# Moving the mLSTM branch's projection from Merge into the prelude of attention, with two of its splits on GpSimd

## The chip, the core and the metric

The kernel runs on one core of a Trainium2 chip. The metric is the device time of one launch in microseconds, as the median of several runs. The core has TensorE (matmuls; PE in the profile), VectorE (DVE), ScalarE (ACT), GpSimd (POOL) and SyncE (SP), which only issues transfers here. ScalarE and GpSimd issue transfers too, each into a queue of its own.

## The reference, cut to what matters

One layer of a hybrid backbone over T = 1152 tokens (128 context, 1024 latent), width D = 1024. Three branches (mLSTM, HGRN2, attention) each make an output of width 512 per token. Merge is then

```
proj_b  = einsum('blnw,nwd->blnd', branches, w_branch)   # n = 3 branches, w = 512, d = 1024
gates_b = sigmoid(bg)
merged  = sum_n(gates_b * proj_b)
x       = x + g1 * (merged @ w_out)
```

and an FFN follows. Everything is float32.

## The kernel before

The phases run one after the other, with a barrier of all engines between them: projection, mLSTM, HGRN2, attention (`attention`, L1452), Merge (`blend`, L1907), FFN (`ffn`, L2198). The two scans and attention write their outputs, features on the partitions, to `y_dram`, 4 x 128 rows for each branch.

**Three passes.** A float32 product is made of three matmuls on operands that are split in two: a high half, which is a copy rounded to TensorE's format (made by ScalarE), and a low half, the operand minus the high half (made by VectorE). `three_passes` (L52) issues high x high, high x low and low x high.

**Merge before.** `blend` multiplies the branches in three stages, n = 0, 1, 2, each of 8 tiles (t) of 128 output features. A tile is 3 column thirds (TH = 384 tokens) x 4 blocks of 128 inputs x 3 passes = 36 matmuls of 128x384, into three banks; two sets of banks alternate. TensorE may start tile m when VectorE has taken tile m-2 (`taken`). VectorE multiplies the banks by the tile's gate (L2088) and adds the product to `merged` (L2092, L2094). The gates are 24 transfers of 576 KB on GpSimd's queue (L1979) into a ring of four buffers, issued as buffers come free; ScalarE makes the sigmoid (L2011). Between tiles ScalarE and VectorE split the operands of the next stage (L1990, L1995, L2063, L2067), and in the last stage the output weights, in quarters (L2000, L2071). The loads come on SP's queue (L1950, L1954). The output projection and the residual follow.

**Stage 0's operands** are loaded in attention: SP issues four transfers of y (L1521) and two of weights (L1523) behind attention's own loads; ScalarE makes the six high halves first of all (L1707, L1710). VectorE makes the low halves in `ahead` (L1873, L1875), when the last query tile's second group begins, ahead of that group's normalisation.

**Attention before.** Its prelude is one chain. VectorE waits for four loads, squares and sums the keys (L1774 to L1778), GpSimd makes the power (L1542), VectorE scales the keys, turns them by the rotary table and splits them (L1785 to L1802). TensorE transposes them (L1588), and ScalarE evicts (L1715). Meanwhile VectorE norms the context's queries. These are transposed (L1568, L1573), then come the context's scores (L1602), their maxima on VectorE, exponentials on ScalarE (L1722), transposes of the probabilities (L1607), the eviction (L1725) and the context's outputs (L1613). Then four rounds: shift scores (L1626), each followed by a reduction on VectorE (L1858) that the next but one waits for at most. Then a loop over 8 query tiles of two groups of heads: nine key blocks each of scores (L1639, L1640), exponential (L1752) and values (L1649), with a normalisation (L1864, L1865) at the end. GpSimd makes the rotary products of the queries (L1556 to L1559) and the powers.

The engines' programs are written out by hand; semaphores carry the order.

Of the kernel before, what the change touches and what calls it, by code (L numbers as in the profile page):

```python
# [21 lines left out]
P = 128  # L22
# [1429 lines left out]
def attention(nc, g):  # L1452
# [14 lines left out]
    with Phase(nc, "att") as ph:  # L1467
# [27 lines left out]
        yt = ph.sb("yt", [P, 4, P])  # L1495
        names = ("load qload const knd kpow kout ktm kte qd qpow rope cpart qtm qte csmm cmx cex cptm cpte comm cdone "
                 "part s1 mx nm ptm pte s2 ex pv on yout kv dve mly mlw mlhi")
# [6 lines left out]
        use = lambda i, k: 2 + 5 * i + k  # L1504

        @block.sync
        def _(sp):
            tok = lambda c, w: g.tok_dram[:, c:c + w].rearrange("(t p) v -> p t v", p=P)
            with nc.allow_non_contiguous_dma(reason="rows of 64 values"):
# [12 lines left out]
            for b in range(2):  # L1522
                sp.dma_start(g.wraw[:, 2048 * b:2048 * b + 2048], io["w_branch"][b]).then_inc(sem["mlw"], 16)  # L1523
# [5 lines left out]
            with sp.Fori(0, 7) as i:  # L1529
                sp.wait_ge(sem["qd"], 4 * i + 8)  # L1530
                sp.dma_start(q[:].rearrange("p h d -> p (h d)"),
                             g.tok_dram[bass.ds(i * P + 2 * P, P), C_AQ:C_AQ + AH * HD]).then_inc(sem["qload"], 16)
            sp.wait_ge(sem["kout"], 32)

        @block.gpsimd
        def _(gp):
# [5 lines left out]
            gp.tensor_tensor(krs[:], kms[:], khalf[:], ALU.pow).then_inc(sem["kpow"], 1)  # L1542
            gp.wait_ge(sem["qd"], 3)
# [33 lines left out]
        def _(pe):  # L1577
            pe.wait_ge(sem["knd"], 6)

            n = 0  # L1580
            for part in range(2):
                rows = (P, H1)[part]
                for kv in range(KV):
                    for t0, nt in ((0, 4), (4, 4), (8, 2)):
# [6 lines left out]
                        n += 1  # L1591
            pe.wait_ge(sem["kte"], 12)
# [5 lines left out]
            mm.then_inc(sem["qtm"], 1)  # L1598
            pe.wait_ge(sem["qte"], 4)
# [4 lines left out]
            mm.then_inc(sem["csmm"], 1)  # L1604
            pe.wait_ge(sem["cex"], 8)
            for c in range(AH):
                mm = pe.transpose(ps[:, 6 + c // G, c % G * P:c % G * P + P], prc[:, c * P:c * P + P], g.ident[:])  # L1607
            mm.then_inc(sem["cptm"], 1)
            pe.wait_ge(sem["cpte"], 1)
# [5 lines left out]
            mm.then_inc(sem["comm"], 1)  # L1615

# [76 lines left out]
            for a in range(G):  # L1693
                shift_scores(0, 0, a)
            shifts(0, 0, 1)
            with pe.Fori(0, 7) as i:
# [7 lines left out]
        def _(act):  # L1704
            act.wait_ge(sem["mly"], 64)
            for k in range(4):
                act.activation(g.ys0[:, k, :], g.ys0[:, 4 + k, :].bitcast(F32), ACT.Copy).then_inc(sem["mlhi"], 1)  # L1707
            act.wait_ge(sem["mlw"], 32)
            for b in range(2):
                act.activation(g.wt[:, b, :], g.wraw[:, 2048 * b:2048 * b + 2048], ACT.Copy).then_inc(sem["mlhi"], 1)  # L1710
            for n in range(12):
# [3 lines left out]
                act.activation(kt[part][0:rows, kv, t0 * P:(t0 + nt) * P], ps[0:rows, n % 6, 0:nt * P], ACT.Copy).then_inc(sem["kte"], 1)  # L1715
            act.wait_ge(sem["qtm"], 1)
            for kv in range(KV):
                act.activation(qt[kv][:], ps[:, kv, :], ACT.Copy).then_inc(sem["qte"], 1)
                act.activation(qm[kv][0:H1, :], ps[0:H1, 2 + kv, :], ACT.Copy).then_inc(sem["qte"], 1)
            act.wait_ge(sem["cmx"], 1)  # L1720
            for c in range(AH):
                act.activation(prc[:, c * P:c * P + P], ps[:, 4 + c // G, c % G * P:c % G * P + P], ACT.Exp,  # L1722
                               bias=mxc[:, c:c + 1], scale=QS).then_inc(sem["cex"], 1)
            act.wait_ge(sem["cptm"], 1)
            act.activation(ptc[:].rearrange("p (a n) -> p a n", a=2), ps[:, 6:8, :], ACT.Copy).then_inc(sem["cpte"], 1)  # L1725
# [19 lines left out]
            def group(i, kv, more):  # L1745
# [3 lines left out]
                for j in range(NT):  # L1749
# [3 lines left out]
                    if j == 3 and kv == 0:  # L1753
                        output(use(i, 1), i)
                if more:
                    shifts(use(i, 2 if kv == 0 else 4), 1 - kv)

            queries(0, 0)
            shifts(1, 0)
            with act.Fori(0, 7) as i:  # L1760
# [5 lines left out]
            act.wait_ge(sem["yout"], 16 * 10)  # L1766

        @block.vector
        def _(v):
            link = Chain(v, sem["dve"])  # L1770
            wide = lambda x, n: x.unsqueeze(2).broadcast_to([P, n, HD])
            flat = lambda x: x.rearrange("p t h d -> p (t h) d")
            v.wait_ge(sem["load"], 64)
# [51 lines left out]

            norm_a(0)
# [80 lines left out]
def blend(nc, g):  # L1907
# [4 lines left out]
    with Phase(nc, "mrg") as ph:  # L1912
        ys = [g.ys0[:], g.zb[:, 0:8 * T].rearrange("p (k t) -> p k t", t=T)]
# [3 lines left out]
        wo = [[g.zb[:, 2 * D * k + D * n:2 * D * k + D * n + D] for n in range(2)] for k in range(4)]  # L1917
# [3 lines left out]
        g1 = g.zf[:, 8 * D:10 * D].rearrange("p (a n) -> p a n", a=2)  # L1921
        h = [g.ys0, g.xb]
# [7 lines left out]
        w_in = [ph.sem(f"w_in{i}") for i in range(2)]  # L1930
        bg_in = [ph.sem(f"bg_in{i}") for i in range(4)]
# [12 lines left out]
        def _(sp):  # L1944
            for n in (1, 2):
                if n == 2:
                    sp.wait_ge(mm_done, 8)
                for k in range(KB):
                    r = (KB * n + k) * P
                    sp.dma_start(ys[n % 2][:, KB + k, :].bitcast(F32), g.y_dram[r:r + P, :]).then_inc(y_in[k], 16)  # L1950
                for s in range(2):
                    if n == 2:
                        sp.wait_ge(w_lo, s + 1)
                    sp.dma_start(raw[s], io["w_branch"][2 * n + s]).then_inc(w_in[s], 16)  # L1954
            for k in range(KD):
                sp.wait_ge(w_lo if k < 4 else wo_lo, 3 + k // 2 if k < 4 else k - 3)
                sp.dma_start(quarter[k % 4], io["w_out"][k * P:k * P + P, :]).then_inc(wo_in[k % 4], 16)
            sp.wait_ge(mm_done, 16)
            for who in range(2):
                sp.dma_start(g1[:, who, :], g.gate_rows[who, 0:D].partition_broadcast(P)).then_inc(g_in, 16)  # L1960
            sp.wait_ge(m_lo, KD)
# [5 lines left out]
            sp.dma_start(g.zf[:, 5 * D + 5 * T:6 * D + 5 * T], io["w_ffn_out"][0:P, :]).then_inc(ahead, 16)  # L1967
# [3 lines left out]
            sp.wait_ge(ahead, 48)  # L1971

        @block.gpsimd
        def _(gp):
            gp.memset(half[:], -0.5).then_inc(pool, 1)
            for n in range(8 * NB):
                if n >= 4:
                    gp.wait_ge(taken, n - 3)
                gp.dma_start(bg[n % 4], g.bg_dram[n * P:n * P + P, :]).then_inc(bg_in[n % 4], 16)  # L1979
# [7 lines left out]
        def _(act):  # L1987
            def branch_hi(n, k):
                act.wait_ge(y_in[k], 16 * n)
                act.activation(ys[n % 2][:, k, :], ys[n % 2][:, KB + k, :].bitcast(F32), ACT.Copy).then_inc(y_hi, 1)  # L1990

            def weight_hi(n, s):
                act.wait_ge(w_in[s], 16 * n)
                act.wait_ge(mm_done, 8 * n + 4 * s - 4)
                act.activation(w[0][s], raw[s], ACT.Copy).then_inc(w_hi, 1)  # L1995

            def out_hi(k):
                act.wait_ge(wo_in[k % 4], 16 * (k // 4) + 16)
                act.wait_ge(mm_done, 16 if k < 4 else 20 if k < 6 else 24)
                act.activation(wo[k][0], quarter[k % 4], ACT.Copy).then_inc(wo_hi, 1)  # L2000

            def merged_hi(k):
                act.wait_ge(summed, k + 1)
                act.wait_ge(mm_done, 24)
                act.activation(h[0][:, k, :], g.merged[:, k, :], ACT.Copy).then_inc(m_hi, 1)

            for n in range(NB):
                for t in range(8):
                    m = 8 * n + t
                    act.wait_ge(bg_in[m % 4], 16 * (m // 4) + 16)  # L2010
                    act.activation(bg[m % 4], bg[m % 4], ACT.Sigmoid).then_inc(bg_sig, 1)  # L2011
# [37 lines left out]
            act.wait_ge(ahead, 48)  # L2049
# [7 lines left out]
        def _(v):  # L2057
            link = Chain(v, dve)

            def branch_lo(n, k):  # L2060
                x = ys[n % 2]
                v.wait_ge(y_hi, KB * (n - 1) + k + 1)
                v.tensor_tensor(x[:, KB + k, :], x[:, KB + k, :].bitcast(F32), x[:, k, :].bitcast(F32), ALU.subtract).then_inc(y_lo, 1)  # L2063

            def weight_lo(n, s):
                v.wait_ge(w_hi, 2 * (n - 1) + s + 1)
# [12 lines left out]
            for n in range(NB):  # L2079
                for t in range(8):  # L2080
                    m = 8 * n + t
                    if n and t == 0:
                        weight_lo(n, 1)
                    v.wait_ge(mm_done, m + 1)
                    v.wait_ge(bg_sig, m + 1)
                    into = g.merged[:, t, :]
                    dst = part[t % 2] if n else into
                    v.tensor_tensor(dst.rearrange("p (a n) -> p a n", a=3), ps[:, 3 * (t % 2):3 * (t % 2) + 3, 0:TH],  # L2088
# [67 lines left out]
        def _(pe):  # L2156
            for m in range(8 * NB):
                n, t, s = m // 8, m % 8, m % 8 // 4
                if n and t == 0:
                    pe.wait_ge(y_lo, KB * n)  # L2160
                if n and t % 4 == 0:
                    pe.wait_ge(w_lo, 2 * (n - 1) + s + 1)
                if m >= 2:
                    pe.wait_ge(taken, m - 1)
# [524 lines left out]
```

## Time and profile before

| | us |
|---|---|
| median of 3 runs | 2627.57 (2626.71 to 2628.74) |
| the profiled execution | 2627.34 |
| its span in the trace | 2625.4 |
| TensorE matmuls busy | 2452.9 (93%) |
| TensorE weight loads busy | 2263.3 (86%) |
| VectorE busy | 1180.9 (45%) |
| ScalarE busy | 680.8 (26%) |
| GpSimd busy | 140.3 (5%) |
| attention, first load to Merge's first matmul | 1176.4 to 1499.4 |

All times of rows are us from the span's start. Matmuls are pipelined, so a single one shows longer than the distance to the next. PEclk is TensorE's granted clock as a share of full speed.

### The profile page before, as it was taken

How to read it: one execution, taken by the hardware profiler on the slowest of the kernel's cores; microseconds unless marked ns; L12 is line 12 of the kernel's file. 1: busy time of each engine (PE TensorE's matmuls, PEld its weight loads, DVE VectorE, ACT ScalarE, POOL GpSimd, SP SyncE). 2: the span in 40 equal slices, each digit the busy share in tenths (PEclk: the TensorE clock that was granted, in tenths of full speed). 3: DMA queues.
4: the chain of work that ended last, by engine and by line, in shares of the span. 5: the costliest groups of instructions: out<-in, count | busy, mean ns of one | idle time of the engine just before them, and what ended most of it. 6: DMA issues, size and time to landing. Idle time of an engine off the chain costs nothing. (4 is left out here: it accounts for less than half of the span.)

```text
span 2625.4 us, 41733 instructions
## 1 busy us (share of the span) xinstructions
PE 2452.9 (93%) x17459; PEld 2263.3 (86%) x17459; DVE 1180.9 (45%) x1749; ACT 680.8 (26%) x1034; POOL 140.3 (5%) x179
## 2 busy tenths in 40 slices
PE   6999999997999789974999999988999999999998
PEld 4887689997999688973999899778999999999997
DVE  3331110102444555645555446554555555555555
ACT  3321111112233223323444333232211211111112
POOL 0000000001100000002111000010000000000000
PEclk8999999998999899995999999998999999999999
DMA  6225422215442532112000154223101110111012
GB/s 254 105 82 200 174 104 94 94 55 178 154 143 80 169 105 97 53 51 97 17 16 16 63 217 162 105 80 120 41 32 48 48 40 32 48 48 39 33 48 81
DMA packets 90780, 237.75 MB, mean 91 GB/s; under 512 B 11904, under 2 KB 49232, under 8 KB 80928
## 3 DMA queue, kind: packets, MB, share of 16 engines
q1 hardware_dynamic: 58464, 169.97, 18.6%
q10 hardware_dynamic: 28224, 50.74, 5.1%
q0 software_dynamic: 3968, 15.21, 1.7%
q8 instruction: 99, 1.62, 0.3%
q14 instruction: 25, 0.20, 0.0%
HBM read 179.13 MB, written 56.83 MB: 90 GB/s over the span
## 5 line engine op out<-in xcount | busy, mean ns | idle before, releaser
L55 PE MATMUL ps<-ys,wt 128*128 128x384 f32 x2688 | 703.3, 337 | 13.2 <-DVEq L2401 9.1
L55 PEld LDWEIGHTS ps<-ys,wt 128*128 128x128 f32 x2688 | 492.9, 189 | 31.0 <-DVEq L2401 9.5
L2354 DVE TENSOR_TENSOR merged<-merged,ps 128x512 f32<-128x512 f32 x378 | 259.5, 687 | 325.3 <-PE ps L55 322.1
L55 PE MATMUL ps<-xb,wt 128*128 128x384 f32 x1056 | 358.6, 340 | 0.0
L55 PE MATMUL ps<-zb 128*128 128x512 f32 x1056 | 298.2, 394 | 0.0
L55 PEld LDWEIGHTS ps<-xb,wt 128*128 128x128 f32 x1056 | 198.5, 188 | 17.2
L55 PEld LDWEIGHTS ps<-zb 128*128 128x128 f32 x1056 | 193.3, 188 | 16.6
L55 PE MATMUL ps<-prj_whi,h_hi 128*128 128x512 f32 (+1 forms) x432 | 165.0, 382 | 7.3 <-DVE h_lo L544 7.3
L55 PE MATMUL ps<-prj_wlo,h_hi 128*128 128x512 f32 (+1 forms) x432 | 162.7, 377 | 0.0
L55 PE MATMUL ps<-prj_whi,h_lo 128*128 128x512 f32 (+1 forms) x432 | 162.5, 376 | 0.0
L55 PE MATMUL ps<-h_hi,prj_whi 128*128 128x384 f32 x480 | 160.5, 334 | 0.8 <-ACT prj_tst L467 0.8
L55 PE MATMUL ps<-h_hi,prj_wlo 128*128 128x384 f32 x480 | 160.5, 334 | 0.0
L55 PE MATMUL ps<-h_lo,prj_whi 128*128 128x384 f32 x480 | 160.4, 334 | 0.0
L529 DVE TENSOR_TENSOR prj_wlo<-prj_raw,prj_whi 128x2048 fp32r<-128x2048 f32 (+1 forms) x22 | 48.1, 2199 | 240.3 <-ACT prj_whi L449 240.2
L1649 PEld LDWEIGHTS ps<-att_va,att_pt 128*128 128x128 f32 x1152 | 145.4, 192 | 6.3
L1649 PE MATMUL ps<-att_va,att_pt 128*128 128x65 f32 x1152 | 144.1, 270 | 0.0
L2286 ACT ACTIVATE zb<-zf 128x384 fp32r<-128x384 f32 x66 | 34.7, 526 | 395.9 <-DVE zf L2375 395.9
L1858 DVE TENSOR_REDUCE att_mx<-ps 128x1 f32<-128x1152 f32 x64 | 86.9, 1358 | 77.0 <-PE ps L1626 76.3
L55 PE MATMUL ps<-h_hi,hgr_gwhi 128*128 128x384 f32 x288 | 103.7, 360 | 12.7 <-DVE hgr_gwlo L687 12.4
L55 PEld LDWEIGHTS ps<-prj_whi,h_hi 128*128 128x128 f32 x432 | 82.6, 191 | 31.6 <-DVE h_lo L544 7.8
L1752 ACT ACTIVATE att_pt<-ps 128x512 f32<-128x512 f32 x144 | 83.5, 597 | 101.6 <-PE ps L1640 95.8
L55 PE MATMUL ps<-h_hi,mls_gwhi 128*128 128x384 f32 x288 | 101.2, 351 | 1.3 <-DVE mls_gwlo L687 1.3
(339 smaller groups left out, 3979.6 us busy)
## 6 DMA issues: line engine op xcount, KB each, us to landing
wraw<-in_w_ffn_in SPq DMA_DIRECT2D x22, 1024.0 KB, 4.8
prj_raw<-in_w_ada SPq DMA_DIRECT2D x16, 1024.0 KB, 6.0
xf<-bg_dram POOLq DMA_DIRECT2D x24, 576.0 KB, 4.1
tok_dram<-prj_tst ACTq DMA_DIRECT2D x45, 256.0 KB, 2.1
feat_dram<-prj_fst ACTq DMA_DIRECT2D x20, 576.0 KB, 2.8
zf<-in_w_ffn_out SPq DMA_DIRECT2D x22, 512.0 KB, 12.6
prj_raw<-in_w_tok SPq DMA_DIRECT2D x10, 1024.0 KB, 6.7
prj_raw<-in_w_feat SPq DMA_DIRECT2D x10, 1024.0 KB, 4.8
```

The costliest lines, as they stand in the source:

```text
L55: mm = pe.matmul(out, lhs[a], rhs[b], start=first and n == 0, stop=last and n == 2)
L529: v.tensor_tensor(w[1][b % 2][:, at], raw[u % NR][:, 0:width], w[0][b % 2][:, at].bitcast(F32), ALU.subtract).then_inc(lo_done, 1)
L1649: mm = pe.matmul(ps[:, OB, a * H1:a * H1 + H1], pt[j % 3][:, a * P:a * P + P], va[:, j, kv, :], start=False, stop=j == NT - 1 and a == G - 1)
L1752: act.activation(pt[j % 3][:], ps[:, ST + j % 3, :], ACT.Exp, scale=QS).then_inc(sem["ex"], 1)
L1858: v.tensor_reduce(mx[:, a % 2:a % 2 + 1], ps[:, 0:3, 0:TH], AX.XY, ALU.max).then_inc(sem["mx"], 1)
L2286: act.activation(a[0][s][:, t * TH:t * TH + TH], gate[:, t * TH:t * TH + TH], ACT.Copy).then_inc(a_hi, 1)
L2354: v.tensor_tensor(dst, dst, ps[:, bank, :], ALU.add).then_inc(added, 1)
```

## The change

Branch 0 (mLSTM) is multiplied in attention's prelude. The work is 24 blocks (`branch`), each one third of one tile: 12 matmuls into bank 6 or 7. Block u is tile 4*(u//12) + u%4, third u%12//4, so blocks 0 to 3 use third 0 of y and the first half of the weights, blocks 4 to 7 third 1, 8 to 11 third 2, and 12 to 23 the second half of the weights. ScalarE evicts each block (`store`) and issues its transfer to `b0_dram` (`put`). TensorE's blocks stand: 10 ahead of the key transposes, 2 behind them, 2 behind the query transposes, 3 behind the context's scores, 2 behind the probabilities' transposes, 1 behind the context's outputs and 4 between the rounds of shift scores. y's loads are by thirds; VectorE makes the low half of third 0 and of both halves of the weights, GpSimd those of thirds 1 and 2. The context's probabilities are transposed into banks 2 and 3 instead of 6 and 7.

Merge has 16 tiles instead of 24 (stages 1 and 2). In stage 1 VectorE first multiplies the stored product by its gate, then the banks by theirs, and adds. So GpSimd's queue brings two gates per tile there, and SP's a stored product. Branch 1's operands are loaded and split in attention: the loads behind the query loads, the high halves in the last query tile, the low halves in `ahead`, as before. The buffers of Merge and of FFN change places; FFN loads its first output weights itself, and multiplies by its gate row in two halves of 512.

```diff
 attention, sync:
+                branch_in(0)
+                branch_w(0)
                 sp.dma_start(kn[:]..., tok(C_AK, KV * HD)).then_inc(sem["load"], 16)
 ...
                 sp.dma_start(tab[:], io["rope"]).then_inc(sem["load"], 16)
+                branch_in(1)
+                branch_in(2)
+                branch_w(1)
 ...
-            for k in range(4):
-                sp.dma_start(g.ys0[:, 4 + k, :].bitcast(F32), g.y_dram[k * P:k * P + P, :]).then_inc(sem["mly"], 16)
-            for b in range(2):
-                sp.dma_start(g.wraw[:, 2048 * b:2048 * b + 2048], io["w_branch"][b]).then_inc(sem["mlw"], 16)
 ...
+            sp.wait_ge(sem["b0mm"], 24)
+            for k in range(4):
+                sp.dma_start(g.ys0[:, 4 + k, :].bitcast(F32), g.y_dram[(4 + k) * P:(5 + k) * P, :]).then_inc(sem["mly"], 16)
+            for b in range(2):
+                sp.dma_start(g.wraw[:, 2048 * b:2048 * b + 2048], io["w_branch"][2 + b]).then_inc(sem["mlw"], 16)
 attention, gpsimd, behind the keys' power:
+            for c in (1, 2):
+                gp.wait_ge(sem["b0yh"], c + 1)
+                at = slice(c * TH, c * TH + TH)
+                gp.tensor_tensor(g.ys0[:, 4:8, at], g.ys0[:, 4:8, at].bitcast(F32), g.ys0[:, 0:4, at].bitcast(F32),
+                                 ALU.subtract).then_inc(sem["b0yl"], 1)
 attention, tensor:
+            def branch(units):
+                for u in units:
+                    t, c = branch_unit(u)
+                    if u % 4 == 0 and u < 12:
+                        pe.wait_ge(sem["b0yl"], c + 1)
+                    if u % 12 == 0:
+                        pe.wait_ge(sem["b0wl"], u // 12 + 1)
+                    if u >= 2:
+                        pe.wait_ge(sem["b0ev"], u - 1)
 ...
+            branch(range(0, 10))
             pe.wait_ge(sem["knd"], 6)
 attention, scalar:
+            def store(units):
+                for u in units:
+                    act.wait_ge(sem["b0mm"], u + 1)
+                    if u >= 3:
+                        act.wait_ge(sem[f"b0out{u % 3}"], 16 * (u // 3))
+                    act.activation(b0st[u % 3][:], ps[:, 6 + u % 2, 0:TH], ACT.Copy).then_inc(sem["b0ev"], 1)
+                    if u:
+                        put(u - 1)
+            branch_hi(0)
+            weight_hi(0)
+            branch_hi(1)
+            branch_hi(2)
+            weight_hi(1)
+            store(range(0, 10))
 ... in group, behind exponential j:
+                    if isinstance(i, int) and kv == 0 and j in (1, 4, 6, 7):
+                        ahead((1, 4, 6, 7).index(j))
+                    if isinstance(i, int) and kv == 1 and j in (1, 4):
+                        ahead(4 + j // 4)
 attention, vector:
+            branch_lo(0)
+            weight_lo(0)
             v.wait_ge(sem["load"], 64)
 ...
+            weight_lo(1)
             norm_a(0)
 blend, sync:
+            for i in range(2):
+                sp.dma_start(done[i], g.b0_dram[i * P:i * P + P, :]).then_inc(done_in[i], 16)
+            ... y and weights of branch 2, the two gate rows g1
+            for i in range(2, 8):
+                sp.wait_ge(taken, 2 * i - 3)
+                sp.dma_start(done[i % 2], g.b0_dram[i * P:i * P + P, :]).then_inc(done_in[i % 2], 16)
 blend, vector:
+            for n in (1, 2):
                 for t in range(8):
+                    if n == 1:
+                        v.wait_ge(done_in[t % 2], 16 * (t // 2) + 16)
+                        v.wait_ge(bg_sig, m)
+                        v.tensor_tensor(into, done[t % 2], bg[(m - 1) % 4], ALU.mult).then_inc(taken, 1)
+                    v.wait_ge(mm_done, 8 * (n - 1) + t + 1)
 blend, tensor:
+            for m in range(16):
 ...
                 if m >= 2:
-                    pe.wait_ge(taken, m - 1)
+                    pe.wait_ge(taken, 2 * m - 2 if m < 10 else m + 7)
```

## Rows read from the trace of the kernel before

**Rows 1.** The page: span, engines' busy time and TensorE's line in 40 slices.

```profile
span 2625.4 us, 41733 instructions
PE 2452.9 (93%) x17459; PEld 2263.3 (86%) x17459; DVE 1180.9 (45%) x1749; ACT 680.8 (26%) x1034; POOL 140.3 (5%) x179
PE   6999999997999789974999999988999999999998
```

**Rows 2.** Windows: length, busy us of PE, PEld, DVE, ACT, POOL, granted clock, DMA share, GB/s.

```profile
1176.40:1200.70 24.30, 0.01 (x1) 0.01 (x1) 15.08 (x24) 7.36 (x6) 3.62 (x4) 0.50 0.79 262
1200.70:1242.50 41.80, 24.68 (x120) 20.68 (x121) 20.10 (x41) 13.92 (x29) 13.54 (x15) 0.62 0.09 22
1200.00:1210.00 10.00, 8.37 (x54) 8.13 (x55) 6.73 (x15) 6.90 (x13) 2.53 (x2) 0.73 0.16 41
1220.00:1230.00 10.00, 6.62 (x26) 5.12 (x24) 2.17 (x7) 1.62 (x2) 5.25 (x7) 0.50 0.10 26
1240.00:1250.00 10.00, 9.12 (x44) 7.51 (x44) 3.48 (x5) 3.58 (x6) 0.00 (x0) 0.69 0.01 2
```

**Rows 3.** Timeline of Merge: start, us, engine, line, operation; VectorE's products and TensorE's first stage.

```profile
1513.47 1.36 DVE L2088 TENSOR_TENSOR merged<-ps,xf 128x1152 f32<-128x1152 f32 x1 [1.89 <-PE ps L55]
...
1557.15 1.36 DVE L2088 TENSOR_TENSOR xf<-ps,xf 128x1152 f32<-128x1152 f32 x1 [1.86 <-PE ps L55]
...
1607.07 1.36 DVE L2088 TENSOR_TENSOR xf<-ps,xf 128x1152 f32<-128x1152 f32 x1 [1.10 <-PE ps L55]
...
1499.38 51.50 PE L55 MATMUL ps<-ys,wt 128*128 128x384 f32 x288 [4.09 <-PEq L75]
```

**Rows 4.** Timeline of attention's prelude: the keys' chain and the first group.

```profile
1183.02 1.36 DVE L1774 TENSOR_TENSOR att_k<-att_kn 128x1152 f32<-128x1152 f32 x1 [13.98 <-DMA att_tab<-in_rope]
...
1186.12 3.25 POOL L1542 TENSOR_TENSOR att_krs<-att_kms,att_khalf 128x18 f32<-128x18 f32 x1 [9.35 <-DVE att_kms L1778]
...
1189.48 1.36 DVE L1785 TENSOR_TENSOR att_kn<-att_kn,att_krs 128x1152 f32<-128x1152 f32 x1 [1.80 <-POOL att_krs L1542]
...
1200.69 4.53 PE L1588 MATMUL ps<-ident,att_kparthi 128*128 128x128 f32 x20 [30.40 <-DVE att_kpartlo L1802]
...
1241.80 1.09 PE L1568 MATMUL ps<-ident,att_qpart 128*128 128x128 f32 x4 [0.88 <-DVE att_qpart L1824]
```

**Rows 5.** Durations by line, ns min/median/max: the splits, GpSimd's multiplies, VectorE's beside the power.

```profile
L1707 ACT ACTIVATE ys<-ys x4: 1147/1147/1164, 1192.7 to 1195.9; 128x1152 fp32r<-128x1152 f32 x4
L1556 POOL TENSOR_TENSOR att_u<-att_qn,att_qtb x16: 735/740/745, 1211.7 to 1431.1; 128x256 f32<-128x256 f32 x16
L1782 DVE TENSOR_TENSOR att_qtab<-att_tab,att_grow x4: 418/425/426, 1185.9 to 1187.3; 128x256 f32<-128x256 f32 x4
```

**Rows 6.** Timeline in mLSTM: GpSimd's two selects and VectorE beside them; that operation's durations.

```profile
648.36 1.21 POOL L823 TENSOR_SCALAR_AFFINE_SELECT mls_ub<-mls_ub 128x1152 f32<-128x1152 f32 x1 [15.26 <-DMA mls_gn<-in_ml_g]
...
649.52 3.52 POOL L823 TENSOR_SCALAR_AFFINE_SELECT mls_ub<-mls_ub 128x1152 f32<-128x1152 f32 x1
...
648.53 3.45 DVE L1006 SCALAR_TENSOR_TENSOR mls_wsb<-mls_q,mls_wsb 128x2304 f32<-128x2304 f32 x1
651.90 1.22 DVE L1019 COPY mls_st<-mls_s 128x129 f32<-128x129 f32 x1
...
L1006 DVE SCALAR_TENSOR_TENSOR mls_wsb<-mls_q,mls_wsb x4: 2557/2558/3448, 648.5 to 811.6; 128x2304 f32<-128x2304 f32 x4
```

**Rows 7.** Merge's start: the sigmoids of gates 0 and 3, and a window of full queues.

```profile
1507.55 1.17 ACT L2011 ACTIVATE xf<-xf 128x1152 f32<-128x1152 f32 x1 [6.93 <-DMA xf<-bg_dram]
...
1519.59 1.17 ACT L2011 ACTIVATE xf<-xf 128x1152 f32<-128x1152 f32 x1 [1.55 <-DMA xf<-bg_dram]
...
1505.00:1510.00 5.00, 5.00 (x31) 5.00 (x30) 1.17 (x1) 2.23 (x2) 0.00 (x0) 1.00 1.04 426
```

**Rows 8.** Attention's tail: the fifth exponential, the weights' low halves, the last normalisation.

```profile
1485.86 0.60 ACT L1752 ACTIVATE att_pt<-ps 128x512 f32<-128x512 f32 x1 [0.76 <-PE ps L1640]
...
1481.84 5.16 DVE L1873 TENSOR_TENSOR ys<-ys 128x1152 fp32r<-128x1152 f32 x4
...
1486.91 4.49 DVE L1875 TENSOR_TENSOR wt<-wraw,wt 128x2048 fp32r<-128x2048 f32 x2
...
1493.93 0.18 DVE L1864 RECIPROCAL att_rs<-ps 128x4 f32<-128x4 f32 x1 [2.54 <-PE ps L1649]
```

More of the change, by code:

```diff
@@ L1495, in attention @@
         yt = ph.sb("yt", [P, 4, P])
+        b0st = [ph.sb(f"b0st{i}", [P, TH]) for i in range(3)]
         names = ("load qload const knd kpow kout ktm kte qd qpow rope cpart qtm qte csmm cmx cex cptm cpte comm cdone "
-                 "part s1 mx nm ptm pte s2 ex pv on yout kv dve mly mlw mlhi")
+                 "part s1 mx nm ptm pte s2 ex pv on yout kv dve mly mlw mlhi b0y0 b0y1 b0y2 b0w0 b0w1 b0yh b0wh b0yl b0wl b0mm b0ev b0out0 b0out1 b0out2")
         sem = {n: ph.sem(n) for n in names.split()}
@@ L1591, in _ @@
                         n += 1
+            branch(range(10, 12))
             pe.wait_ge(sem["kte"], 12)
@@ L1598, in _ @@
             mm.then_inc(sem["qtm"], 1)
+            branch(range(12, 14))
             pe.wait_ge(sem["qte"], 4)
@@ L1615, in _ @@
             mm.then_inc(sem["comm"], 1)
+            branch(range(19, 20))
             def queries(u, kv):
@@ L1694, in _ @@
                 shift_scores(0, 0, a)
+                branch(range(20 + a, 21 + a))
             shifts(0, 0, 1)
+            pe.wait_ge(sem["b0ev"], 24)
             with pe.Fori(0, 7) as i:
@@ L1715, in _ @@
                 act.activation(kt[part][0:rows, kv, t0 * P:(t0 + nt) * P], ps[0:rows, n % 6, 0:nt * P], ACT.Copy).then_inc(sem["kte"], 1)
+            store(range(10, 12))
             act.wait_ge(sem["qtm"], 1)
@@ L1719, in _ @@
                 act.activation(qm[kv][0:H1, :], ps[0:H1, 2 + kv, :], ACT.Copy).then_inc(sem["qte"], 1)
+            store(range(12, 14))
             act.wait_ge(sem["cmx"], 1)
@@ L1754, in group, with ahead @@
                         output(use(i, 1), i)
+                    if isinstance(i, int) and kv == 0 and j in (1, 4, 6, 7):
+                        ahead((1, 4, 6, 7).index(j))
+                    if isinstance(i, int) and kv == 1 and j in (1, 4):
+                        ahead(4 + j // 4)
                 if more:
                     shifts(use(i, 2 if kv == 0 else 4), 1 - kv)
+            def ahead(n):
+                if n == 0:
+                    act.wait_ge(sem["mly"], 64)
+                if n == 4:
+                    act.wait_ge(sem["mlw"], 32)
+                if n < 4:
+                    act.activation(g.ys0[:, n, :], g.ys0[:, 4 + n, :].bitcast(F32), ACT.Copy).then_inc(sem["mlhi"], 1)
+                else:
+                    b = n - 4
+                    act.activation(g.wt[:, b, :], g.wraw[:, 2048 * b:2048 * b + 2048], ACT.Copy).then_inc(sem["mlhi"], 1)
             queries(0, 0)
+            store(range(20, 24))
             shifts(1, 0)
+            put(23)
             with act.Fori(0, 7) as i:
@@ L1766, in _ @@
             act.wait_ge(sem["yout"], 16 * 10)
+            for i in range(3):
+                act.wait_ge(sem[f"b0out{i}"], 16 * 8)
         @block.vector
@@ L1920, in blend @@
         part = [g.xf[:, 4 + i, :] for i in range(2)]
-        g1 = g.zf[:, 8 * D:10 * D].rearrange("p (a n) -> p a n", a=2)
-        h = [g.ys0, g.xb]
+        done = [g.xf[:, 6 + i, :] for i in range(2)]
+        g1 = g.zf[:, 8 * T:8 * T + 2 * D].rearrange("p (a n) -> p a n", a=2)
+        h = [wide, g.xb]
+        g.h = h
         free = g.merged[:].rearrange("p k t -> p (k t)")
@@ L1930, in blend @@
         w_in = [ph.sem(f"w_in{i}") for i in range(2)]
+        done_in = [ph.sem(f"done_in{i}") for i in range(2)]
         bg_in = [ph.sem(f"bg_in{i}") for i in range(4)]
@@ L2003, in merged_hi, with gate @@
                 act.wait_ge(summed, k + 1)
-                act.wait_ge(mm_done, 24)
+                act.wait_ge(mm_done, 16)
                 act.activation(h[0][:, k, :], g.merged[:, k, :], ACT.Copy).then_inc(m_hi, 1)
-            for n in range(NB):
+            def gate(m):
+                act.wait_ge(bg_in[m % 4], 16 * (m // 4) + 16)
+                act.activation(bg[m % 4], bg[m % 4], ACT.Sigmoid).then_inc(bg_sig, 1)
+            for n in (1, 2):
                 for t in range(8):
-                    m = 8 * n + t
-                    act.wait_ge(bg_in[m % 4], 16 * (m // 4) + 16)
-                    act.activation(bg[m % 4], bg[m % 4], ACT.Sigmoid).then_inc(bg_sig, 1)
+                    if n == 1:
+                        gate(2 * t)
+                        gate(2 * t + 1)
+                    else:
+                        gate(16 + t)
                     if n < 2:
@@ L2048, in _ @@
                     split(i - 1)
-            act.wait_ge(ahead, 48)
+            act.wait_ge(ahead, 32)
             act.wait_ge(o_mm, NT)
@@ L2156, in _ @@
         def _(pe):
[L2157 to L2162, printed above, removed]
+            for m in range(16):
+                n, t, s = 1 + m // 8, m % 8, m % 8 // 4
+                if n == 2 and t == 0:
+                    pe.wait_ge(y_lo, KB)
+                if n == 2 and t % 4 == 0:
+                    pe.wait_ge(w_lo, s + 1)
                 if m >= 2:
-                    pe.wait_ge(taken, m - 1)
+                    pe.wait_ge(taken, 2 * m - 2 if m < 10 else m + 7)
                 ws = [x[s].rearrange("p (k n) -> p k n", k=KB) for x in w]
@@ L2237, in _ @@
             sp.sem_inc(w_in, 32)
[L2238 to L2239 removed]
+            sp.dma_start(oraw, io["w_ffn_out"][0:P, :]).then_inc(o_in, 16)
+            for n in range(2):
+                sp.dma_start(g2[n], g.gate_rows[1, D + 512 * n:D + 512 * n + 512].partition_broadcast(P)).then_inc(g2_in, 16)
             for i in range(0, LAT // P, 4):
```

130 lines of the change are left out of this document (77 added, 53 removed).

## The prediction

> **What bounds the kernel now.** I read the page first. TensorE's matmuls cover 93% of the span, and the slices show where they do not [rows 1]. The windows then divide the stretch that the change touches [rows 2]. From 1176.4 to 1200.7 us TensorE does nothing at a granted clock of 0.50 (the lower level, 1.2 GHz). To 1242.5 it is busy 24.7 of 41.8 us at a mean clock of 0.62. After that the attention loop fills it. The third view is the order of work in Merge [rows 3]: its three stages of 288 matmuls run without a gap. The same product of tile 0 comes at 1557.15 in the stage of branch 1 and at 1607.07 in that of branch 2, so a stage costs 49.92 us at the full clock, and one of its 24 blocks of 12 matmuls costs 2.08 us. So the end is set by TensorE's work, and what moves into its idle 41 us before the loop is gained, less what it pushes back.
>
> **Removed.** Stage 0 of Merge: 49.9 us off the path. The slow start of a stage stays, since the next one now starts there. Merge's gated product of branch 0 stays on VectorE but now reads SBUF.
>
> **The prelude up to the key transposes.** Before, the chain is: loads landed 1183.0, VectorE works on the keys, GpSimd's power 3.25 us in between, VectorE again from 1189.5, and the transposes at 1200.69 [rows 4]. Three things are put ahead.
>
> Loads. SP's queue now starts with 0.79 MB of y and 1.05 MB of weights. In Merge large loads move 426 GB/s [rows 7], so these cost 4.4 us, and the four loads of the keys' chain land at about 1187.4. ScalarE's and VectorE's pieces come first on VectorE. From ScalarE's 1.15 us for 1152 elements [rows 5] and VectorE's 2.25 for 2048 [rows 8], in proportion, I take 1.5 and 1.7 us for 1536, and 1.9 for ScalarE's 2048. With y landed at about 1180.3 and weights at 1182.8 (at that rate from a first packet near 1178.4): ScalarE to 1181.8 and 1184.7, VectorE to 1183.5 and 1187.0. This is just under the keys' loads, so both together cost +4.4 us, bounded by 3 and, if VectorE starts its keys after later pieces, 8.
>
> GpSimd's two pieces (y thirds 1 and 2). The nearest rows are its multiplies of 256 elements at 0.74 us [rows 5]; by these 1536 cost 4.4 us each. Below, the one-input select of 1152 elements takes 1.21 us [rows 6], or 1.6 us for 1536. I take 4.4, as the operation is the same kind with two inputs. GpSimd's power for the keys ends at 1193.7, so the pieces start there, just where VectorE's second part wants to start. Do they run together? The trace has the case [rows 6]. While GpSimd runs its first select, from 648.36 for 1.21 us, a VectorE operation with two SBUF inputs takes 3.45 us; the other three of its form take 2.56. GpSimd's second select then takes 3.52 us, ending after the VectorE one, and the copy behind it on VectorE takes 1.22 us, for 129 elements. So each waits for the other's whole instruction. Only the power of 18 elements leaves VectorE alone: four multiplies run beside it at 0.42 us each [rows 4, 5]. The keys' chain is nearly all two-input operations, so I take both pieces as added to it: 11.2 us of chain (1189.48 to 1200.69) from 1193.9, plus 8.7, ends at 1213.8.
>
> The Trainium skill says the same under SBUF — State Buffer, "Who interferes with whom": a VectorE instruction with two SBUF inputs and a GpSimd one that reads SBUF share a read interface, and the second to issue waits fully. By that rule the trace agrees (3.52 against 1.21 us). The Trainium skill's page GPSIMD Engine Reference, in the comparison of elementwise operations at 2048 elements, gives 4497 ns for the two-input add; as an estimate that is 3.4 us for 1536, and by it the chain would end 2 us earlier.
>
> TensorE meanwhile starts ten blocks at 1187.0. Blocks 0 to 3 take 8.3 us plus 1.6 for the slow start (Merge's first 72 matmuls end at 1513.47, 14.1 us after 1499.38 against 12.5 at full clock [rows 3]), to 1197.0. Block 4 waits for GpSimd's first piece (1198.1) and block 8 for its second, which queues behind one VectorE operation of 1.4 us (1204). Blocks 8 and 9 end at 1208.5. So the transposes wait for VectorE, not for the blocks: 1213.8, **+13.1 us**. If GpSimd's pieces did not hold VectorE, they would start when the blocks let them, at about 1208.5 to 1211, so the hold is worth 3 to 5 us, not 8.7.
>
> **From the transposes to the first group.** Before: 1200.69 to 1241.80, 41.1 us [rows 4]. After, step by step on TensorE, with its own work halved where it ran at 0.50: key transposes 7.2 us (set by ScalarE's twelve evictions, as before), query transposes 1.8, the context's scores 1.9, its probabilities' transposes 1.1, its outputs 1.9, the first query transposes with their eviction 1.3, four rounds of shift scores 4 x 0.7, the shift's transposes and the split that the first group waits for 1.5. That is 19.5. Fourteen blocks are 29.1. One wait remains: block 16 needs block 14's eviction, which ScalarE makes only behind eight exponentials, 0.8 us. Everything else that TensorE waited for (weights' low half 2.3 us ahead of the query norm on VectorE, the softmax, the four reductions of 1.36 us) is shorter than the blocks laid over it. The sum is 49.4, or **+8.3**. The evictions (24 of about 0.5 us) and their stores (24 issues of 0.39 us) lie in ScalarE's idle time, with 13.9 us busy of 41.8 [rows 2].
>
> Group 0 then starts with a clock already full. Before, 1240 to 1250 had 0.69 [rows 2], about 6 us at the lower level, some 4 of them in the group: **-1.5**.
>
> **The attention's tail.** Branch 1's halves are now made there. ScalarE's six pieces sit behind exponentials 1, 4, 6, 7 of the last tile's first group and 1, 4 of its second. A piece of 1.15 to 1.9 us fits before the next exponential is needed by the values. But VectorE's `ahead` waits for the sixth: exponential 4 ends at 1486.46, its piece at 1488.4, then VectorE's four pieces of 1.3 and the 4.49 us of the weights to 1498.1, and only then the last normalisation, which was at 1493.93 [rows 8]. Behind it stand the last transposes, the eviction, the store and Merge: **+4.2**.
>
> **Merge's first stage.** It now needs two gates and one stored product per tile. Gate 0 landed at 1507.55 and gate 3 at 1519.59, and the queues are full there at 426 GB/s [rows 7]; gate 1, between them in order, was in time for tile 1's product at 1513.47 [rows 3], so tile 0 is taken about then, when tile 2's matmuls may begin. Tile 1 needs gate 3: sigmoid to 1520.8, product to 1522.1, where tile 3 should start at 1519.7, so it waits 2.5 us. The queues are full some 6 us longer (6.7 MB of SP's instead of 4.5, and the gates), until about 1526; tile 2 is taken at 1528.6, when it is wanted. I take **+2.7**; ends 0 and 8 (every load late). VectorE has 3 x 1.36 + 1.36 us per 6.24, with 6.4 us once, so it keeps up. FFN's first output weights and its gate row are loaded later but behind a first step of tens of us: nothing; its product in two halves adds 0.1 us to VectorE per step, under TensorE's cover.
>
> **Sum.** -49.9 + 13.1 + 8.3 - 1.5 + 4.2 + 2.7 = -23.1. The profiled execution took 2627.3 us (span 2625.4), 0.2 under the median of 2627.57; from it, 2604 us.
>
> **Rivals.**
> - A, lighter preparation: GpSimd's pieces cost 1.6 to 3.4 us, or do not hold VectorE. Against it stand rows 6. Then -3 to -5: 2600.
> - B, loads are the limit: Merge's first stage asks for 19.7 MB in 50 us (24 gates and products of 0.59, y 2.36, weights 2.1, gate rows 1.05), 393 GB/s, near the 426 seen, and the keys' loads stand behind 1.84 MB. For it: full queues for 15 us even before. Against: 5.5 MB of it is for later; once that is in, a tile needs 1.77 MB in 6.24 us, 284 GB/s. Price +5 (first loads slower, at the 262 GB/s of the prelude [rows 2]) to +10: 2609 to 2614.
> - C, slower than before: TensorE's clock stays at the lower level through the prelude because its work is broken by waits. A block then costs 4.2 us and all 24 add 49.9: 2654. It decides once more than 11 blocks run so (11 x 2.08 = 23). For it: from 1220 to 1230 the engine was 6.6 us busy and still at 0.50 [rows 2]. Against: 1200 to 1210, 8.4 busy, 0.73, and with blocks laid in the waits few gaps pass 2 us. A few blocks so give 2606 to 2612.
> - D, the gain does not come: another wait hides what is saved. TensorE ran all three stages without a gap, so I see none; and the moved blocks are truly left out of Merge.
>
> **Chances.** Forecast 0.55, A 0.14, B 0.17, C 0.06 (0.04 past its point), D 0.02, and 0.06 for several small delays to 2612. The range holds the forecast with its bounds, all of A and most of B: 2596 to 2613. Measurement tells 0.2% (5 us) from no change. Faster by more is all but C's far part and D: 0.94; within 0.2% 0.02; slower 0.04.
>
> **What would show it.** Transposes of the keys at about 1214 (1209 if nothing is held), the first group at about 1263, full clock from the first ten blocks on; GpSimd's two subtractions at 3.4 to 4.4 us with VectorE multiplies beside them lengthened; the last normalisation some 4 us after the last values; one wait of 2 to 3 us ahead of tile 3 of Merge's first stage; Merge some 47 us shorter. It is wrong if the blocks show 4 us each, if the first stage has gaps at every tile, or if the keys' chain starts well past 1188.

## The result and the profile after

| | before | with the change |
|---|---|---|
| median of 4 runs, us | 2628.15 (2626.71 to 2630.21) | 2613.67 (2608.53 to 2620.26) |
| ratio, 95% interval | | 0.9939 (0.9925 to 0.9953) |
| profiled execution, its span | 2627.34, 2625.4 | 2620.26, 2618.4 |
| the changed kernel again, 5 runs, beside 9 of before | 2631.06 | 2610.18, ratio 0.992 (0.9906 to 0.9933) |

So the change is worth 16 us in the first set (2628.15 x 0.0061) and 21 in the second (2631.06 x 0.008). I had forecast 23. The profiled execution is the slowest of its four and gains only 7. The reason lies ahead of the change, and has to be taken out first. The page of the changed kernel:

```profile
span 2618.4 us, 41825 instructions
PE 2457.1 (94%) x17459; PEld 2268.4 (87%) x17459; DVE 1182.6 (45%) x1768; ACT 690.6 (26%) x1057; POOL 148.3 (6%) x181
```

TensorE's count of 17459 is that of before [rows 1]: nothing was left out. Now HGRN, whose instructions are the same in both. The windows from its first matmul to attention's first load, one of the kernel before and one of the changed:

```profile
864.50:1176.30 311.80, 277.85 (x5276) 263.12 (x5276) 177.24 (x343) 96.46 (x179) 14.86 (x20) 0.95 0.27 89
```

```profile
864.50:1184.90 320.40, 282.50 (x5276) 267.45 (x5276) 177.22 (x343) 96.56 (x179) 14.85 (x20) 0.93 0.26 86
```

(Both in the order of [rows 2].) The counts agree, VectorE and ScalarE were busy as long, but the granted clock was 0.93 instead of 0.95, TensorE's matmuls took 4.7 us more, and the phase was 8.6 us longer. I therefore compare stages from attention's first load on, SP's first transfer there (1176.37 before, 1184.95 after). In microseconds:

| stretch | before | after | change | forecast |
|---|---|---|---|---|
| ahead of attention's first load | 1176.4 | 1184.9 | +8.6 | 0 |
| first load to key transposes | 24.3 | 41.2 | +16.8 | +13.1 |
| key transposes to first scores of the loop | 41.9 | 45.3 | +3.5 | +8.3 |
| loop, to the last group's values | 240.1 | 238.5 | -1.6 | -1.5 |
| from there to the last normalisation | 11.3 | 15.2 | +3.8 | +4.2 |
| last normalisation to Merge | 5.4 | 6.0 | +0.5 | 0 |
| Merge to its output projection | 156.6 | 117.7 | -39.0 | -47.2 |
| the rest | 969.4 | 969.7 | +0.3 | 0 |

The last seven changes sum to -15.6 us (from unrounded times). The gain missing from the forecast is in Merge.

**Merge.** The timeline's TensorE rows of both stages:

```profile
1531.03 27.73 PE L55 MATMUL ps<-ys,wt 128*128 128x384 f32 x144 [4.17 <-PEq L75]
1566.23 27.25 PE L55 MATMUL ps<-ys,wt 128*128 128x384 f32 x144 [7.48 <-DVE xf L2206]
1593.32 50.09 PE L55 MATMUL ps<-zb,wt 128*128 128x384 f32 x288
```

Before, the first stage ran through [rows 3]. Now it stops for 7.5 us in its middle, ahead of tile 4, on a product of VectorE. Who VectorE waited for stands in the list of waits from 1531 to 1660:

```profile
DVE merged L2203 <- DMA xf<-b_dram: 9.3, 1, 9.3
...
PE ps L55 <- DVE xf L2206: 7.5, 1, 7.5
```

VectorE waited for the stored product of tile 2, which landed 32.5 us after Merge's start. Windows of tile 0 (before, then after) and of tile 4 (after):

```profile
1499.40:1507.00 7.60, 7.60 (x36) 7.60 (x37) 0.00 (x0) 1.22 (x1) 2.29 (x5) 0.81 0.86 326
```

```profile
1531.00:1539.70 8.70, 8.68 (x36) 8.70 (x36) 0.00 (x0) 1.84 (x2) 2.34 (x5) 0.68 0.89 337
1566.20:1574.60 8.40, 8.37 (x36) 8.37 (x37) 8.29 (x7) 2.86 (x3) 1.61 (x3) 0.74 0.93 328
```

A tile takes 6.24 us at full clock. Behind its wait tile 4 takes 8.4 at a mean clock of 0.74, and tile 0 a microsecond more than before at 0.68. So the stop costs 7.5 + 2.1, and the start 1.2: 10.9 of the 49.9 us given back, where I had 2.7. The start's part may be chance: from the first matmul of tile 0 to the first of tile 1 the four profiles of the kernel before show 7.6, 7.7, 9.0 and 9.1 us, and this one 8.9.

**The prelude.** Timeline, TensorE, up to the key transposes:

```profile
1196.55 6.92 PE L55 MATMUL ps<-ys,wt 128*128 128x384 f32 x24 [17.69 <-DVE wt L1866]
1206.90 19.37 PE L55 MATMUL ps<-ys,wt 128*128 128x384 f32 x96 [3.43 <-ACT att_b0st L1760]
1226.11 1.14 PE L1625 MATMUL ps<-ident,att_kparthi 128*128 128x128 f32 x9
```

and the other engines there:

```profile
1199.42 3.25 POOL L1557 TENSOR_TENSOR att_krs<-att_kms,att_khalf 128x18 f32<-128x18 f32 x1 [14.07 <-DVE att_kms L1882]
...
1202.64 7.97 POOL L1561 TENSOR_TENSOR ys<-ys 128x1536 fp32r<-128x1536 f32 x2
1202.78 4.51 DVE L1889 TENSOR_TENSOR att_kn<-att_kn,att_krs 128x1152 f32<-128x1152 f32 x1 [1.80 <-POOL att_krs L1557]
1204.56 1.91 ACT L1771 ACTIVATE wt<-wraw 128x2048 fp32r<-128x2048 f32 x1 [2.64 <-DMA wraw<-in_w_branch]
...
1206.38 0.85 ACT L1760 ACTIVATE att_b0st<-ps 128x384 f32<-128x384 f32 x2
...
1207.33 4.50 DVE L1890 TENSOR_TENSOR att_kn<-att_kn,att_grow 128x1152 f32<-128x1152 f32 x1
...
1218.68 1.56 DVE L1906 TENSOR_TENSOR att_kpartlo<-att_kr,att_kparthi 128x640 fp32r<-128x640 f32 x2
```

Both of VectorE's multiplies that lie beside GpSimd's pieces took 4.5 us instead of 1.36, which the first had before [rows 4]. So the hold is there, 6.3 us of it, and the keys' chain ended at 1220.2, 35.3 us after the first load. But the transposes did not start then. They started at 1226.11, right behind the ten blocks. The blocks were late: the first two took 6.92 us, and then came a wait of 3.4 us for ScalarE's eviction of block 0 (L1760). The evictions stand in ScalarE's order behind the high half of the weights' second half (L1771), which waited for its load until 1204.56. From the transposes to the first group TensorE is full, at full clock:

```profile
1226.10:1271.10 45.00, 43.36 (x286) 42.56 (x285) 17.98 (x38) 19.92 (x43) 12.04 (x14) 1.00 0.26 86
```

**The tail.** The six high halves and what waits for the last of them:

```profile
1513.63 1.90 ACT L1843 ACTIVATE wt<-wraw 128x2048 fp32r<-128x2048 f32 x1
...
1515.56 5.16 DVE L1978 TENSOR_TENSOR ys<-ys 128x1152 fp32r<-128x1152 f32 x4 [6.36 <-ACT wt L1843]
...
1525.05 0.18 DVE L1969 RECIPROCAL att_rs<-ps 128x4 f32<-128x4 f32 x1
```

VectorE idles 6.4 us for the sixth piece, and the last normalisation comes 15.2 us after the last group's first values, where it was 11.3 [rows 8].

### The profile page after: what moved, and what is told of

It is laid out like the page before. It is cut to its first block and busy times, and to the rows that moved or that the text cites. A ratio compares the mean times of both kernels' runs of the same rounds, so it can differ in the third digit from the quotient of the medians.

```text
span 2618.4 us, 41825 instructions
## 1 busy us (share of the span) xinstructions
PE 2457.1 (94%) x17459; PEld 2268.4 (87%) x17459; DVE 1182.6 (45%) x1768; ACT 690.6 (26%) x1057; POOL 148.3 (6%) x181
## 5 line engine op out<-in xcount | busy, mean ns | idle before, releaser
L55 PE MATMUL ps<-zb,wt 128*128 128x384 f32 x2400 | 651.5, 337 | 9.1 <-DVEq L2522 9.1
L55 PEld LDWEIGHTS ps<-zb,wt 128*128 128x128 f32 x2400 | 441.7, 188 | 26.8 <-DVEq L2522 9.5
L55 PE MATMUL ps<-ys 128*128 128x512 f32 x1056 | 298.2, 394 | 0.0
L55 PEld LDWEIGHTS ps<-ys 128*128 128x128 f32 x1056 | 193.3, 187 | 16.6
L55 PE MATMUL ps<-ys,wt 128*128 128x384 f32 x576 | 112.5, 357 | 32.8 <-DVE wt L1866 17.7
L2406 ACT ACTIVATE ys<-zf 128x384 fp32r<-128x384 f32 x66 | 34.7, 526 | 395.6 <-DVE zf L2496 395.6
L55 PEld LDWEIGHTS ps<-ys,wt 128*128 128x128 f32 x576 | 109.0, 204 | 34.4 <-issue 22.6
L55 PE MATMUL ps<-h_hi,hgr_gwhi 128*128 128x384 f32 x288 | 105.4, 366 | 12.6 <-DVE hgr_gwlo L687 12.4
```

Of the source, the lines that this page charges most:

```text
L55: mm = pe.matmul(out, lhs[a], rhs[b], start=first and n == 0, stop=last and n == 2)
L2406: act.activation(a[0][s][:, t * TH:t * TH + TH], gate[:, t * TH:t * TH + TH], ACT.Copy).then_inc(a_hi, 1)
```

## The experiments

Experiments 1 to 7 and 9 run the changed kernel, with the edit shown; 8, 10 and 11 run the kernel before. The first four ran beside 9 runs of the kernel before (2631.06 us), the next four beside 9 (2627.53), the last three beside 9 (2627.79).

**1. The changed kernel again** (no edit).

> The changed kernel once more, as the control of this set. In its first profile HGRN, which runs before anything that the change touches, ended 8.6 us later than in the kernel before, with the granted clock at the lower level in more stretches. Theory (chance): the lapses of the clock differ between executions; then this profile shows another time for HGRN (0 to 9 us against before) and the ratio to before lies at 0.992 to 0.996. Rival (placement): the new stored tensor or the longer program makes HGRN slower each time; then it is again 8 to 9 us late.

2610.18 us, ratio 0.992 (0.9906 to 0.9933). HGRN took 315.1 us, not 320.5. The stages behind attention's first load came out as in the first profile to 0.1 us, but for the blocks ahead of the transposes (39.3 us instead of 41.2). There the first 24 matmuls took 6.10 us instead of 6.92, and the next 96 18.52 instead of 19.37. That speaks for chance; experiments 8, 10 and 11 look at it from the other side.

**2. Merge's loads in another order.**

```diff
-            for s in range(2):
-                sp.dma_start(raw[s], io["w_branch"][4 + s]).then_inc(w_in[s], 16)
-            for who in range(2):
-                sp.dma_start(g1[:, who, :], ...).then_inc(g_in, 16)
             for i in range(2, 8):
                 sp.wait_ge(taken, 2 * i - 3)
                 sp.dma_start(done[i % 2], ...).then_inc(done_in[i % 2], 16)
+                if i in (2, 3):
+                    sp.dma_start(raw[i - 2], io["w_branch"][2 + i]).then_inc(w_in[i - 2], 16)
+                if i in (4, 5):
+                    sp.dma_start(g1[:, i - 4, :], ...).then_inc(g_in, 16)
```

> Only the order of SP's loads in Merge's first stage is changed: the weights of branch 2 follow the stored products of tiles 2 and 3, the gate rows those of tiles 4 and 5. Theory: tile 4's wait of 7.8 us and the slow matmuls behind it (2.1 us) come from the stored product of tile 2 landing 32.5 us after Merge's start behind 4.5 MB of other loads; the wait shrinks to under 1 us and Merge is 8 to 10 us shorter than with the change as it is. Rival: the gates on GpSimd's queue are the limit (gate 5 landed at 25.7); then a wait of 3 to 6 us stays at tile 3 or 4.

2600.85 us, ratio 0.9887 (0.9872 to 0.9902). Merge to its output projection: 108.3 us instead of 117.6. TensorE's first stage runs through:

```profile
1520.11 53.12 PE L55 MATMUL ps<-ys,wt 128*128 128x384 f32 x288 [4.17 <-PEq L75]
1573.07 50.08 PE L55 MATMUL ps<-zb,wt 128*128 128x384 f32 x288
```

The order of SP's queue was the cause. The gates were not the limit, and neither was the bandwidth: no wait at tile 3 or 4 is left, though the queues were as full (392 GB/s in the first 32.6 us, where the changed kernel had 387 up to the landing of tile 2's product).

**3. ScalarE's order in the prelude.**

```diff
             branch_hi(2)
+            store(range(0, 4))
             weight_hi(1)
-            store(range(0, 10))
+            store(range(4, 10))
```

> Only ScalarE's order in the prelude is changed: the high half of the weights' second half is made behind the evictions of blocks 0 to 3 instead of ahead of them. Theory: TensorE's wait of 3.4 us at block 2 and the slow matmuls behind it (2.7 us) come from an eviction queued behind a weight load that landed at 1204.5; without it blocks 2 to 9 end 5 to 6 us earlier and the key transposes start 35 us after the first load instead of 41. Rival: GpSimd's two pieces, and VectorE's chain held by them, are the real bound; then the transposes gain at most 1 us.

2606.62 us, ratio 0.991 (0.9895 to 0.9926). The transposes start 35.6 us after the first load (39.3 to 41.6 in the five profiles with the order as it was):

```profile
1186.70 23.69 PE L55 MATMUL ps<-ys,wt 128*128 128x384 f32 x120 [17.66 <-DVE wt L1867]
1210.74 1.42 PE L1625 MATMUL ps<-ident,att_kparthi 128*128 128x128 f32 x11 [0.35 <-DVE att_kpartlo L1907]
```

The ten blocks run through in 23.7 us, and what ends the wait at the transposes is VectorE's chain again, 0.35 us behind them. The interval of the whole kernel overlaps with experiment 1's, so the gain of 3.7 to 6.0 us rests on the stage's times.

**4. The tail.**

```diff
-                v.wait_ge(sem["mlhi"], 6)
+                v.wait_ge(sem["mlhi"], 4)
                 ... four low halves of y
                 for b in range(2):
+                    v.wait_ge(sem["mlhi"], 5 + b)
                     ... low half of the weights
```

> Only VectorE's wait in the attention's tail is changed: the low halves of y wait for four high halves, those of the weights each for its own, instead of all for six. Theory: the last normalisation returns to 12.6 us after the last group's start (it was 16.5), and the kernel is 4 us shorter. Rival: the order of ScalarE's pieces among the exponentials costs something itself; then less than 2 us comes back.

2604.88 us, ratio 0.9901 (0.9886 to 0.9916). The last normalisation is again 11.3 us behind the last group's first values, 3.8 us earlier. The rows of this kernel: VectorE's two parts end before TensorE's last values, which it then waits for as before.

```profile
1497.80 5.16 DVE L1978 TENSOR_TENSOR ys<-ys 128x1152 fp32r<-128x1152 f32 x4
...
1502.87 4.49 DVE L1981 TENSOR_TENSOR wt<-wraw,wt 128x2048 fp32r<-128x2048 f32 x2
...
1509.90 0.18 DVE L1969 RECIPROCAL att_rs<-ps 128x4 f32<-128x4 f32 x1 [2.54 <-PE ps L1691]
```

(My expectation gave 12.6 and 16.5 us, counted from the normalisation of the group before; it names the same 3.8 to 3.9 us.) ScalarE's pieces among the exponentials cost nothing that shows in this stage. The interval of the whole kernel overlaps with experiment 1's here too.

**5. The two pieces on VectorE.**

```diff
 gpsimd:
-            for c in (1, 2):
-                ... the two subtractions
 vector, ahead of the wait for the keys' power:
+            branch_lo(1)
+            branch_lo(2)
```

> The changed kernel with the two pieces on VectorE instead of GpSimd, ahead of its keys' multiplies. Theory: the pieces hold VectorE's two-input operations for their whole length (4.50 us instead of 1.36, twice: 6.3 us), and cost VectorE 1.76 us each if it makes them itself; so the keys' chain ends at 32.5 to 33 us after the first load instead of 35.3, but the key transposes stay at 39 to 41.5, since the ten blocks end there: no difference in time. Rival: the keys' chain set the transposes; then they come 2.5 us earlier.

2612.56 us, ratio 0.9943 (0.9925 to 0.9962). The keys' chain ended 30.8 us after the first load, earlier than I expected:

```profile
1193.21 3.43 DVE L1867 TENSOR_TENSOR ys<-ys 128x1536 fp32r<-128x1536 f32 x2
...
1196.56 1.35 DVE L1886 TENSOR_TENSOR att_kn<-att_kn,att_krs 128x1152 f32<-128x1152 f32 x1
1197.94 1.36 DVE L1887 TENSOR_TENSOR att_kn<-att_kn,att_grow 128x1152 f32<-128x1152 f32 x1
```

The two pieces take 3.4 us together, and half of that lies in the 1.8 us that VectorE waits for GpSimd's power anyway. Its multiplies are back at 1.36. The transposes still start at 40.4, behind the blocks, within the 39.3 to 41.6 of the kernels with the pieces on GpSimd. So the split onto GpSimd cost VectorE's chain 4.5 us (35.3 against 30.8), and by the stage's times the kernel nothing. The ratio says no more than that: its interval overlaps with both of those without the edit.

**6. Both, 3 and 5.** The edits of 3 and 5.

> ScalarE's order of the third experiment and the two pieces on VectorE. There the blocks ended at 35.3 and the keys' chain at 35.6. Theory: the chain now ends at 33, the blocks at 35, so the transposes start at about 35.3: 0.3 us earlier than in the third experiment. Rival: VectorE delivers the low halves later than GpSimd did and block 4 or 8 waits; then 36 or more.

2607.92 us, ratio 0.9922 (0.9904 to 0.9941). The chain ended at 31.0 (33 expected), and the transposes start at 35.3, right behind the blocks: 0.3 us ahead of experiment 3, as forecast.

**7. The edits of 2, 3 and 4.**

> The three changes of experiments 2 to 4 together, with the pieces on GpSimd. Theory: the three waits lie behind each other, so their gains add: 9.3 us in Merge, 4 to 6 in the prelude, 3.8 in the tail; ratio to before 0.984 to 0.987. Rival: one of them is taken up by the next wait; ratio over 0.988.

2592.64 us, ratio 0.987 (0.9848 to 0.9891). By stages the gains add: transposes at 36.1, the last normalisation 11.3, Merge 108.0. TensorE's busy time from the first load on shows where the rest lies. Of these 81.8 us it is busy 66.7, and 11.7 of the 15.1 idle ones lie ahead of its first block:

```profile
1176.00:1212.10 36.10, 22.78 (x120) 22.17 (x120) 25.51 (x26) 12.77 (x15) 11.71 (x6) 0.79 0.68 223
1212.10:1257.80 45.70, 43.93 (x287) 42.87 (x288) 22.00 (x42) 19.51 (x42) 13.68 (x15) 1.00 0.26 86
```

**9. The same with both pieces on VectorE.**

> The three changes of experiment 7 and the two pieces on VectorE. Theory: in experiment 7 the keys' chain ended at 36.1 us and the blocks at 35.0, so the pieces on GpSimd cost about 1 us there; here the transposes start at 35.0 to 35.3 and the ratio to before is 0.983 to 0.988. Rival: VectorE's earlier end is worth more than 1 us further on, in the query chain behind it; then the first group starts 2 us or more earlier than in experiment 7 (81.8 us after the first load).

2589.21 us, ratio 0.9854 (0.9836 to 0.9873): the fastest, though its interval overlaps with experiment 7's. The first scores come 79.8 us after the first load instead of 81.8: 1.7 us at the transposes (34.4, where I expected 35.0 to 35.3) and 0.3 behind them. In experiment 7 the transposes waited for VectorE's chain, which ended at 36.1, behind blocks that ended at 35.0; here they start right behind the blocks, which were another 0.4 us earlier (the wait at block 2 was 0.21 us instead of 0.51). So the rival's figure came, but not by its reason. Experiments 3 and 6 are the same pair in the prelude, and there the pieces on GpSimd cost 0.3 us: 0.3 to 1.7 is what two pairs show.

**8, 10 and 11. The kernel before, with a profile each.**

> The kernel before, once more with a profile, for the spread of what runs ahead of the change. Theory (chance): HGRN takes another time than the 311.9 us of the first profile, within the 309.7 to 320.5 us of the profiles so far, while each stage behind the first load of attention agrees within 1 us. Rival: the kernel before is always at 312, and the change makes HGRN unsteady.

> The kernel before with another profile, for HGRN's time alone (311.9 and 310.1 us so far, against 309.7 to 320.5 with the change). Theory (chance): it lies anywhere in 309 to 321. Rival (the change makes it unsteady): again 310 to 312.

> As the last one: the kernel before, for HGRN's time. Chance: 309 to 321. Rival: 310 to 312.

2624.02, 2623.40 and 2628.32 us. HGRN took 310.1, 309.2 and 313.5 us beside 311.9. In the nine profiles with branch 0 moved it took 309.7 to 315.8, and 320.5 once. The ranges overlap, and one long phase in nine is no effect of the change that I could show; that there is none stays open as well, since the four of before never exceeded 313.5, and four of the nine did (middle values 311.0 and 313.2). Behind attention's first load the four profiles of before agree within 0.7 us in the prelude and within 1.5 in Merge, where experiment 8 expected 1.

## Why the prediction came out as it did

The direction was right and the forecast gain too large: ratio 0.9939 and 0.992, or 2612 and 2607 us from 2627.57, where I said 2604, in a range of 2596 to 2613. The raw median of the first set, 2613.67, lies 0.7 us above that range.

- **Removed.** 49.9 us a stage holds: stage 2 took 50.09 for 288 matmuls, as before.
- **Loads and VectorE's first pieces.** Forecast +4.4, measured +4.7 (the keys' chain starts 11.4 us after the first load instead of 6.7; pieces of 1.48, 1.91, 1.76 and 2.29 us). It starts right behind VectorE's second piece, without a wait.
- **GpSimd's pieces.** The hold is as forecast in kind: each piece lengthens one multiply of VectorE, by 3.15 us. The size was off: 3.44 us for the first piece, where I took 4.4 from multiplies of 256 elements. So the chain ended at 35.3 us and not 37.4. The estimate of 3.4 us from the comparison of elementwise operations in the Trainium skill's GPSIMD Engine Reference was the nearer one. I had put the worth of the hold at 3 to 5 us; it was nothing here (experiment 5) and 0.3 to 1.7 once the blocks were earlier (6 and 9). Rival A's condition, pieces of 3.4 us, was met, and its gain did not come, since the blocks set the start of the transposes.
- **The step that failed in the prelude** is the sentence that blocks 0 to 3 run on to 1197.0 and that the transposes wait for VectorE, not for the blocks. It counted TensorE's inputs, not its outputs. Block 2 needs a free bank, so block 0's eviction, and ScalarE had that behind a load that I had myself put at the end of the queue. The wait was 3.4 us, and with the slow matmuls on both sides of it the blocks took 29.6 us instead of 21.5. Of these 8.1 us, 2.1 are an error of my sum: six blocks from 1198.1 on end at 1210.6, not at 1208.5. Experiment 3 undoes the wait: 35.6.
- **Transposes to the first group.** Forecast +8.3, measured +3.8 between the same two matmuls as in the forecast (1226.11 to 1271.06, 44.95 us). The term that was mis-sized is the 7.2 us for the key transposes "set by ScalarE's evictions": at full clock they took 4.3, and the evictions kept up. That is 2.9 of the 4.5 us; the rest is spread over the smaller steps. The whole is 14 blocks and TensorE's own work with 1.6 us of idle time, so the claim that nearly all waits lie under blocks is right.
- **The loop** gave 1.6 us back (1.5 said): its first 7.5 us had a mean granted clock of 0.75 before, and 1.00 after. **The tail** cost 3.8 (4.2 said), and experiment 4 gives it back. Both mechanisms held.
- **The step that failed in Merge**, and the larger one, is "tile 2 is taken at 1528.6, when it is wanted". I put the end of the burst at 26 us after Merge's start, from 6.7 MB of SP's and the gates. But the product of tile 2 stands behind all of SP's loads in one queue, and eight gates landed ahead of it: 12 MB by 32.5 us. Tile 3, where I expected the wait, had none. Rival B said late loads and 5 to 10 us; it came to 8.2 more than the forecast's 2.7, of which 1.2 is the start. Its figure came, but it blamed the bandwidth, and experiment 2 moves the same bytes in another order at the same rate and has no wait. What I lacked was a rival for the order in the queue.
- **Rival C** did not come. The clock was full from the transposes to the first group (mean 1.00), and lower only in the first blocks.
- The two errors ahead of the loop cancel (+3.7 and -4.8); what stands is Merge's 8.2, and small differences of -0.1, -0.4, +0.5 and +0.3 elsewhere.

## What to carry to other kernels

When work is moved into an idle stretch, follow its outputs as closely as its inputs: the free bank, the eviction, and what stands ahead of that eviction in its engine's order. Here a product of 0.59 MB landed 32.5 us after Merge's start, behind 6.7 MB of its own queue and eight gates of another, and the stage ran through once the loads for later stood behind it. So count what stands ahead of a load in its queue, and put the loads that the next steps need ahead of prefetches. An expected gain is best split by stages anchored at a point that both kernels share: here 8.6 us ahead of the change, which no run ties to it, hid half of the gain in one profile.

## What the runs showed of the hardware

- The same HGRN phase, with the same instructions and the same busy times of VectorE and ScalarE, took 309.2 to 320.5 us in 13 profiles. The granted clock stood at 0.95 in one at 311.9 and at 0.93 in the one at 320.5. My forecast had taken the time ahead of the change as fixed.
- Behind a wait of 7.5 us in dense matmuls the next tile took 2.1 us more than its 6.24, at a mean granted clock of 0.74; in the five other profiles with this wait it took 1.5 to 1.9 more. In the five profiles with a wait of 3.1 to 4.6 us behind the second block of the prelude, the ten blocks ran 3.5 to 6.2 us above their 20.8 at full clock, the wait not counted. In the four where that wait is gone or at most 0.5 us (experiments 3, 6, 7 and 9) they ran 2.0 to 3.1 above.
- GpSimd's two-input subtraction of 128x1536 float32 took 3.44 us, and VectorE's multiply beside it 4.51 instead of 1.36; GpSimd's second subtraction, begun while that multiply still ran, took 4.56. GpSimd's power of 18 elements (3.25 us) left VectorE's multiplies beside it at 0.42 us, in both kernels.
